# A two-layer hybrid decoder trunk: the small groups, the memory transposes and half the key projection of the mixer stage in another order

## The reference

```python
z = rmsnorm(x, mix_pre_g) @ w_in                 # 256 x 1024 @ 1024 x 3088
rq, rk, rv, rg, gq, gk, gv, ga, gg = split(z)
ro = retention(rope(rq), rope(rk) * 64**-0.5, rv)        # 4 heads, fixed decay, chunks of 128
ro = rmsnorm(ro) * silu(rg)
log_a = log_sigmoid(ga @ w_a2 + b_a2) / 16
go = gla(gq * 64**-0.5, gk, gv, log_a)                   # 4 heads, gated, causal
go = rmsnorm(go) * silu(gg)
x = x + rmsnorm(concat(ro, go) @ w_out, mix_post_g)

m = rmsnorm(mem, xa_mem_g)                               # 256 memory tokens
q = rmsnorm(x, xa_pre_g) @ w_q
k, v = split(m @ w_kv)                                   # 1024 columns each
x = x + rmsnorm(softmax(q k^T / 16) v @ w_o, xa_post_g)
```

## Time and profile before

| | |
|---|---|
| median of 3 executions | 1249.93 us (1248.46 to 1251.76) |
| the profiled execution, its own time | 1250.62 us |
| its span, first to last instruction | 1248.8 us |
| TensorE busy | 1214.5 us (97%) |
| VectorE busy | 801.1 us (64%) |
| ScalarE busy | 670.1 us (54%) |
| GpSimd busy | 153.7 us (12%) |
| mean granted clock of TensorE | 0.989 |

### The profile page before, as it was taken

One profiled execution on the slowest core, in us unless ns is written; L12 is line 12 of the kernel. 1 busy time (PEld: TensorE's weight loads), 2 busy tenths in 40 slices (PEclk: granted clock), 3 DMA queues, 4 the chain that ended last, 5 costly groups with the idle time before them and its releaser, 6 DMA issues.

```text
span 1248.8 us, 19448 instructions
## 1 busy us (share of the span) xinstructions
PE 1214.5 (97%) x6120; PEld 1017.2 (81%) x6120; DVE 801.1 (64%) x1214; ACT 670.1 (54%) x1117; POOL 153.7 (12%) x282
## 2 busy tenths in 40 slices
PE   7999999998999999999999999999899999999997
PEld 5888888777898888888888888877779988888886
DVE  6766546766756576665476665567667557767655
ACT  6655436644655466553466553456457546555444
POOL 1000003642210010000010000037322001000001
PEclk9999999989999999999999999998999999999999
DMA  8556564442563355565465565463345544555563
GB/s 332 199 172 217 182 212 164 135 135 106 183 201 129 123 191 194 176 211 192 157 204 194 174 211 191 158 214 103 102 169 163 168 159 135 203 175 195 180 213 130
DMA packets 32916, 220.06 MB, mean 176 GB/s; under 512 B 4272, under 2 KB 4528, under 8 KB 8768
## 3 DMA queue, kind: packets, MB, share of 16 engines
q1 hardware_dynamic: 32544, 218.98, 51.2%
q10 hardware_dynamic: 288, 0.02, 0.0%
HBM read 217.93 MB, written 1.05 MB: 175 GB/s over the span
## 4 chain that ended last, share of the span: by engine, by line
PE 89%; DVE 4%; issue 2%; POOL 2%; ACT 1%; DMA 1%; DVEq 0%; ACTq 0%; SPq 0%; POOLq 0%
PE acc L465 27%; PE acc L467 27%; PE acc L466 26%; PE tb L524 3%; DVE w_lo L1182 2%; PE mb L615 1%; PE acc L774 1%; PE mb L758 1%; DMA raw<-in_gu 1%; PE mb L711 1%; ACT w_hi L870 1%; DVE pg L1316 0%; POOL r_head L1679 0%; PE mb L713 0%; DVE xT_lo L1188 0%
## 5 line engine op out<-in xcount | busy, mean ns | idle before, releaser
L1182 DVE SCALAR_TENSOR_TENSOR w_lo<-raw,gains,w_hi 128x512 fp32r<-128x512 f32 x580 | 416.3, 779 | 46.5 <-ACT w_hi L870 45.4
L465 PE MATMUL acc<-w_hi,xT_hi 128*128 128x512 f32 x1024 | 411.3, 402 | 8.4 <-DVE w_lo L1563 4.0
L467 PE MATMUL acc<-w_hi,xT_lo 128*128 128x512 f32 x1024 | 402.7, 393 | 0.0
L466 PE MATMUL acc<-w_lo,xT_hi 128*128 128x512 f32 x1024 | 402.2, 393 | 0.0
L870 ACT ACTIVATE w_hi<-raw,gains 128x512 fp32r<-128x512 f32 x580 | 369.9, 714 | 40.4 <-PE acc L467 40.2
L465 PEld LDWEIGHTS acc<-w_hi,xT_hi 128*128 128x128 f32 x1024 | 194.4, 190 | 51.3 <-DVE xT_lo L1188 5.1
L467 PEld LDWEIGHTS acc<-w_hi,xT_lo 128*128 128x128 f32 x1024 | 194.1, 190 | 41.7
L466 PEld LDWEIGHTS acc<-w_lo,xT_hi 128*128 128x128 f32 x1024 | 194.6, 190 | 37.8
L1176 DVE TENSOR_TENSOR w_lo<-raw,w_hi 128x1024 fp32r<-128x1024 f32 x112 | 123.6, 1145 | 72.6 <-ACT w_hi L864 71.9
L935 ACT ACTIVATE th<-acc,r_half 128x256 f32<-128x256 f32 x88 | 41.7, 474 | 197.3 <-PE acc L467 196.9
L864 ACT ACTIVATE w_hi<-raw 128x1024 fp32r<-128x1024 f32 x112 | 105.4, 991 | 77.2 <-PE acc L467 77.2
(11 more groups left out here) (175 smaller groups left out, 1250.2 us busy)
## 6 DMA issues: line engine op xcount, KB each, us to landing
raw<-in_gu SPq DMA_DIRECT2D x92, 1024.0 KB, 5.2
raw<-in_down SPq DMA_DIRECT2D x32, 1024.0 KB, 5.0
raw<-in_in SPq DMA_DIRECT2D x24, 1024.0 KB, 5.1
raw<-in_kv SPq DMA_DIRECT2D x16, 1024.0 KB, 5.2
raw<-in_down SPq DMA_DIRECT2D x16, 768.0 KB, 4.1
raw<-in_out SPq DMA_DIRECT2D x8, 1024.0 KB, 5.1
raw<-in_q SPq DMA_DIRECT2D x8, 1024.0 KB, 5.2
raw<-in_o SPq DMA_DIRECT2D x8, 1024.0 KB, 5.1
```

Source lines behind the costliest of these rows:

```text
L465: pe.matmul(o, st_hi, mv_hi, start=first, stop=False)
L466: pe.matmul(o, st_hi, mv_lo, start=False, stop=False)
L467: return pe.matmul(o, st_lo, mv_hi, start=False, stop=last)
L1182: dve.scalar_tensor_tensor(w_lo[:, slot, k, :], raw[:, slot, k, :], gains[:, ds(g, 1)], w_hi[:, slot, k, :].bitcast(F32), ALU.mult, ALU.su ...
```

## The change

The work is the same, the order is another. In words:

- TensorE: from pass 4 to pass 9 there is one small group in the middle of a pass (at `k == 4`, so between its two halves) and one behind it. The retention scores come first, then the levels one by one. `ro` stands in the middle of pass 10, `go` behind it. The memory transposes stand inside pass 10. The mixed transposes go by group of heads and not by half of the tokens: retention's behind pass 11, gla's between the two column passes of the first half of the keys.
- One chunk of keys (`C_K0`) is taken ahead of `w_out`, the other (`C_K1`) stays behind it, with the transposes of the new x behind and inside its passes.
- VectorE's and ScalarE's lists follow: one `split_after` between two `level_out` mostly; the squares and the scaling of the memory tokens, and their splitting, come into the projection. GpSimd's `mem_norm` moves to between the levels.
- SyncE loads the memory tokens behind chunk `C_IN + 3`, when x is updated after the first block (`s_x`), into the buffer `yg`; `kT`, `qT` and the probabilities' buffer trade places in memory.

```diff
+C_K0 = len(CHUNKS)
+CHUNKS += [("kv", 0, 0, 4, G_MEM)]
 C_OUT = len(CHUNKS)
 CHUNKS += [("out", c, 0, 4, G_HEAD) for c in range(2)]
-C_K = len(CHUNKS)
-CHUNKS += [("kv", c, 0, 4, G_MEM) for c in range(2)]
+C_K1 = len(CHUNKS)
+CHUNKS += [("kv", 1, 0, 4, G_MEM)]
...
-T_USES += [("mix", t, a) for t, a in XUSE]
 T_USES += [("mem", t, a) for t, a in XUSE]
+T_USES += [("mix", t, a) for a in range(2) for t in range(TT)]
...
-M_USES = ["z", "diag", "lv0", "lv1", "lv2", "rj0", "lv3", "rj1", "lv4", "lv5", "ro", "lv6", "lv7", "go",
+M_USES = ["z", "diag", "rj0", "rj1", "lv0", "lv1", "lv2", "lv3", "lv4", "lv5", "lv6", "lv7", "ro", "go",
           "s0", "s1"]
...
-            kT = sb("kT", [P, KD, TOK], F32, region)
+            qT = sb("qT", [P, KD, TOK], F32, region)
             vx = sb("vx", [P, TT, D], F32, region)
-            mem_t = sb("mem_t", [P, TT, D], F32, region)
+            p_t = sb("p_t", [P, TT, D], F32, region)
...
+        mem_t = yg
...
-                    if ci == C_K:
-
-                        sp.wait_ge(s_of, l * 4 + 4)
-                        sp.dma_start(mem_t[:, :, :], a["mem"].rearrange("(t p) d -> p t d", p=P)).then_inc(s_mem, 16)
-                    if ci == C_K + 3:
+                    if ci == C_V:
                         load_post_gain(l, 2)
                     load(l, ci)
+                    if ci == C_IN + 3:
+
+                        sp.wait_ge(s_x, l * 16 + 8)
+                        sp.dma_start(mem_t[:, :, :], a["mem"].rearrange("(t p) d -> p t d", p=P)).then_inc(s_mem, 16)
...
+                inside = {4: {4: diagonal}, 5: {4: lambda: retention_scores(0)}, 6: {4: lambda: level(l, 0)},
+                          7: {4: lambda: level(l, 2)}, 8: {4: lambda: level(l, 4)}, 9: {4: lambda: level(l, 6)},
+                          10: {2: lambda: mem_transposes(l, 0), 4: retention_outputs,
+                               6: lambda: mem_transposes(l, 1)}}
+                behind = {4: rqk_transposes, 5: lambda: retention_scores(1), 6: lambda: level(l, 1),
+                          7: lambda: level(l, 3), 8: lambda: level(l, 5), 9: lambda: level(l, 7),
+                          10: gated_outputs, 11: lambda: mixed_transposes(l, 0)}
+                for n in range(4, 12):
+                    c, t = n // 2, n % 2
+
+                    def step(k):
+                        if k in inside.get(n, {}):
+                            inside[n][k]()
+                    chunk_pass(l, C_IN + c, Q_IN + c, t, xT_hi, xT_lo, before_k=step)
+                    behind[n]()
...
-                mixed_transposes(l, 0, (1,))
+                wait_split(("mem", 1, 1), l)
+                column_pass(l, C_K0, Q_K0, 0, mT_hi, mT_lo)
+                mixed_transposes(l, 1)
+                column_pass(l, C_K0, Q_K0, 1, mT_hi, mT_lo)
...
-                pair(l, C_OUT, (Q_OUT, Q_OUT + 1), (xT_hi, xT_lo), before_k={0: mix_split(0), 2: mix_split(1)},
-                     mids={0: lambda: mixed_transposes(l, 1), 1: lambda: mem_transposes(l, 0),
-                           2: lambda: mem_transposes(l, 1)})
-
-                wait_split(("mem", 1, 1), l)
-                for t in range(TT):
-                    column_pass(l, C_K, Q_K, t, mT_hi, mT_lo)
-                    x_transposes(l, 2, t)
-                for t in range(TT):
-                    column_pass(l, C_K + 1, Q_K + 1, t, mT_hi, mT_lo)
+                pair(l, C_OUT, (Q_OUT, Q_OUT + 1), (xT_hi, xT_lo), before_k={0: mix_split(0), 2: mix_split(1)})
+                column_pass(l, C_K1, Q_K1, 0, mT_hi, mT_lo)
+                x_transposes(l, 2, 0)
+                column_pass(l, C_K1, Q_K1, 1, mT_hi, mT_lo, mid=lambda: x_transposes(l, 2, 1))
                 wait_x(l, 2, 1)
```

ScalarE's list, from the second half of gla v on:

```diff
                 project(2, 1, v_tok[:, 1, COL:2 * COL], r_8)
                 split_after(5)
+                act.wait_ge(s_mem, l * 16 + 16)
+                for t in range(TT):
...
+                    act.activation(junk_x[:, :], mem_t[:, t, :], ACT.Square,
+                                   accum_out=mss[:, t:t + 1]).then_inc(s_msq, 1)
                 exp_decay(l, 4)
                 project(3, 0, v_tok[:, 0, 0:COL], r_pre)
...
                 exp_decay(l, 6)
-                gate_tanh(4, 0)
                 split_after(8)
                 exp_decay(l, 7)
+                gate_tanh(4, 0)
+                split_after(9)
+                gate_tanh(4, 1)
+                split_after(10)
+                mem_hi(l, 0)
                 head_outputs(l, "ro", 0)
-                gate_tanh(4, 1)
-                split_after(9)
+                mem_hi(l, 1)
+                gate_tanh(5, 0)
                 head_outputs(l, "go", 1)
...
+                split_after(11)
                 gate_tanh(5, 1)
...
+                mix_hi(l, 0)
+                split_hi(l, C_OUT, 1)
```

VectorE's list, from behind the diagonal on, and GpSimd's:

```diff
-                split_after(3)
-                split_after(4)
-                level_out(0)
-                level_out(1)
+                split_lo(l, C_IN + 3, 0, ks=(0, 1))
                 for t in range(TT):
                     t_copy(l, ("rqk", t), rT[:, :, t * P:(t + 1) * P])
+                split_lo(l, C_IN + 3, 0, ks=(2, 3))
+                retention_mask(0)
+                split_after(4)
+                retention_mask(1)
+                level_out(0)
                 split_after(5)
+                level_out(1)
+                split_after(6)
                 level_out(2)
-                split_after(6)
-                retention_mask(0)
+                split_after(7)
                 level_out(3)
-                split_after(7)
-                retention_mask(1)
-                gate_z(4, 0)
+                split_after(8)
                 level_out(4)
                 level_out(5)
-                split_after(8)
+                for t in range(TT):
+                    dve.wait_ge(s_rmem, l * 2 + t + 1)
+                    dve.tensor_scalar(mem_t[:, t, :], mem_t[:, t, :], r_mem[:, t:t + 1], None,
+                                      ALU.mult).then_inc(s_memn, 1)
+                gate_z(4, 0)
+                level_out(6)
+                split_after(9)
+                level_out(7)
+                gate_z(4, 1)
+                split_after(10)
+                mem_lo(l, 0)
                 head_squares("ro", 0)
-                gate_z(4, 1)
-                level_out(6)
-                level_out(7)
-                split_after(9)
+                mem_lo(l, 1)
+                gate_z(5, 0)
                 head_squares("go", 1)
                 for t in range(TT):
                     mixed(4, t)
...
+                split_after(11)
                 gate_z(5, 1)
...
+                mix_lo(l, 0)
+                for t in range(TT):
+                    mixed(5, t)
+                split_lo(l, C_OUT, 1)
...
                     decayed(l, n)
                     if n + 2 < 8:
                         exponents(l, n + 2)
+                    if n in (3, 4):
+                        mem_norm(l, n - 3)
```

More of the change, by code:

```diff
@@ L617, in level, with mixed_transposes @@
                                 mm.then_inc(s_m[e], 1)
-            def mixed_transposes(l, t, groups=(0, 1)):
-                for g in groups:
+            def mixed_transposes(l, g):
+                for t in range(TT):
                     pe.wait_ge(s_mixed, l * 4 + 2 * g + t + 1)
@@ L1073, in mix_out, with mem_hi, mix_hi, copy_out @@
                                    accum_out=mss[:, t:t + 1]).then_inc(s_msq, 1)
+                exp_decay(l, 4)
+                project(3, 0, v_tok[:, 0, 0:COL], r_pre)
+                split_after(6)
+                exp_decay(l, 5)
+                project(3, 1, v_tok[:, 1, 0:COL], r_pre)
+                split_after(7)
+                exp_decay(l, 6)
+                split_after(8)
+                exp_decay(l, 7)
+                gate_tanh(4, 0)
[3 more added lines that the diff above has]
+                mem_hi(l, 0)
+                head_outputs(l, "ro", 0)
+                mem_hi(l, 1)
+                gate_tanh(5, 0)
+                head_outputs(l, "go", 1)
+                split_after(11)
+                gate_tanh(5, 1)
+                mix_hi(l, 0)
+                split_hi(l, C_OUT, 1)
+            def mem_hi(l, t):
+                for g in range(2):
+                    t_hi(l, ("mem", t, g), mT_hi[:, 4 * g:4 * g + 4, t * P:(t + 1) * P])
+            def mix_hi(l, g):
+                for t in range(TT):
+                    t_hi(l, ("mix", t, g), xT_hi[:, 4 * g:4 * g + 4, t * P:(t + 1) * P])
+            def copy_out(l, q, t, dst):
+                wait_pass(l, q, t)
+                act.activation(dst, acc[q % 2][t][:, :], ACT.Copy).then_inc(s_accf[bank(q, t)], 1)
+            def mix_out(l):
+                copy_out(l, Q_K0, 0, kT[:, 0:2, :])
+                mix_hi(l, 1)
+                split_hi(l, C_OUT + 1, 0)
+                copy_out(l, Q_K0, 1, kT[:, 2:4, :])
+                split_hi(l, C_OUT + 1, 1)
                 y_square(l, 1, Q_OUT, 0, 0)
-                mem_hi(l, 0)
```

(24 more changed lines are left out.)

297 lines of the change are left out of this document (122 added, 175 removed).

## The result

The changed kernel takes **1229.3 us** (median of four executions, 1228.6 to 1229.7) against 1249.5 us for the kernel before on the same chip (1248.5 to 1251.8). The ratio is 0.9839, with a 95% interval of 0.9827 to 0.9851: 20 us faster. The forecast was 1226 us, in a range of 1221 to 1238 us.

A forecast was written before the change was run, and what follows sets the result against it. TensorE, busy 97% of the span, was taken as the bound. From 1250.6 us, 17.3 us idle and 11 us clock go, 4.0 us of new waits come, 0.7 us off for the median: 1226 us, range 1221 to 1238 us.

The forecast's parts named there:

- What was to be won: In the mixer stages of both layers: 17.3 us of TensorE's idle time plus 11 us of clock, at most 28.3 us.
- Which waits go: TensorE's waits of 1.95, 1.23 and 1.76 us per layer, shorter ones among the groups, `xT_lo` (1.73 us) and `mem_t` (0.6 us).
- Two prices: VectorE's scaling of the memory tokens at 2 x 0.75 us, and one `level_out` per step at 0.79 us.
- The new waits: TensorE ahead of levels 0, 3 and 4: 0.2 + 0.3 + 1.5 = 2.0 us per layer, none from level 5 on.
- The clock: In the mixer stages, the 11 us lost at the lower clock were all to go, with none lost anew.
- groups set apart by half a pass keep it: Between passes 4 and 10: small groups with half a pass between them keep full clock; a wait among small groups costs it.
- The sum: 17.3 us idle and 11 us clock go, 2 x 2.0 us come: 24.3 us off 1250.6 us; 1225.6 us as median.
- A: Rival: clock still falls behind the new wait ahead of level 4, or in pass 10; 11 us stay, 1237 us; chance 0.15.
- B: Rival: VectorE bounds the mixer stage, 5 us of waits a layer, no clock lost: 1232 us; chance 0.20.
- C: Rival: the chopped stretch, passes 4 to 11, runs at half clock and the kernel gets slower: 1280 us; chance 0.04.
- D: Rival: VectorE's splits and GpSimd's instructions exclude each other fully, 13 us of waits a layer: 1248 us; chance 0.03.

The follow-up runs named there:

- Kernel 2: The changed kernel with level_out(3) moved ahead of split_after(7) and level_out(4) ahead of split_after(8) in VectorE's list: 1222.2 us, ratio 0.9788.
- experiment 5: The changed kernel with w_out's two chunks ahead of both key chunks, as in the kernel before; new order of small groups and memory tokens kept: 1239.4 us.
- experiment 3: The changed kernel with split_after(7) ahead of project(3, 1) in ScalarE's list, VectorE's list as it was: 1224.8 us, ratio 0.9804.
- experiment 6: The changed kernel with GpSimd's instructions from level 2 on cut to the first block of each decayed operand, leaving out computation: 1224.2 us, ratio 0.9809.
- experiment 4: The changed kernel with level 4 behind pass 8, next to level 5, and no group inside pass 8: 1230.1 us, ratio 0.9846.
- experiment 8: The kernel before with level_out(0) moved between split_after(3) and split_after(4) in VectorE's list, nothing else: 1242.4 us, ratio 0.9955.
- experiment 7: Kernel 2 with TensorE made to wait ahead of w_out's second and fourth pass until the pass before has been read: 1235.3 us, ratio 0.9903.
- experiment 1: The changed kernel with only level_out(3) moved ahead of split_after(7) in VectorE's list: 1231.3 us, ratio 0.9859.

## Why the prediction was nearly right, point by point

- **What was to be won: right.** It said 17.3 + 11 = 28.3 us. Kernel 2, which loses nothing in the stage, ends 28.3 us earlier by its span, with 16.9 us of idle time and 11.4 us of busy time, which is the clock's. The terms are off by 0.4 us each, and that they cancel to the decimal is luck.
- **Which waits go: right.** `pgx`, `xT_lo` and `mem_t` are gone, and the banks of `ro` and level 7 are waited for no more, nor are GpSimd's operands of level 0. `xT_lo` went because of the key chunk (experiment 5). The squares, the scaling and the memory transposes cost nothing that TensorE shows: kernel 2 has them all and no wait. Two prices were off without effect: the scaling ran beside GpSimd at 1.0 us an instruction and not 0.75 us, and `level_out` of levels 6 and 7 took 1.33 us and not 0.79 us.
- **The new waits: right in sum and at level 4, wrong in the small ones.** Forecast 4.0 us, measured 2.6 + 1.9 = 4.5 us. At level 4 it was 1.9 us a layer where 1.5 us was worked out, by the named cause, ScalarE's projection (experiment 3), together with the splits' slowing beside GpSimd (experiment 6). The 0.2 and 0.3 us ahead of levels 0 and 3 did not come; 0.67 us at level 5 came in layer 0, where "no more waits" was forecast, since four splits took 4.19 us there.
- **The clock: this term was mis-sized.** It was put at nothing, and the step that failed is "groups set apart by half a pass keep it". The fall behind level 4 in layer 1 came with half a pass ahead of the group and half a pass behind it; its window lacks 25 x 0.07 = 1.7 us. Against kernel 2 the changed one is busy 1205.5 - 1203.1 = 2.4 us longer, so the clock gave back at least 9.0 us of its 11.4 us; the 0.7 us that the window doesn't show were not placed. The reason under that step, that a wait costs the clock when it stands among small groups, does not hold as a rule: the same neighbourhood gave a fall in one layer and none in the other (experiment 4). What it is worth as a tendency is said below. Kernel 2, which has no wait in the stage, has no fall there.
- **The sum.** 0.5 us more of waits and 2.4 us more of busy time make 2.9 us: 1250.6 - 28.3 + 4.5 + 2.4 = 1229.2 us, and the profiled execution took 1229.1 us. The 0.7 us that was taken off for the median fell away, since this time the profiled execution lay 0.2 us below the median. Together that is the distance of 3.7 us between 1225.6 and 1229.3 us.
- **The rivals.** A (1237 us) came true behind one of the three waits that were left, and at a fifth of its price. B (1232 us, waits in every step) did not: levels 0 to 3 did not wait. C is refuted by the mean clock of 0.998. D is refuted as it was priced: no 13 us of waits came.

**What D had wrong is its price.** It added 2.7 us of splits and GpSimd's 3.5 us a level to 6.2 us. But the 3.5 us holds GpSimd's own waiting for VectorE, so the blocking was counted twice. The two timelines of the changed kernel show it:

```profile
259.06 0.73 POOL L1672 TENSOR_TENSOR gqk<-gT,o_sb 128x256 f32<-128x256 f32 x1
...
262.25 0.87 POOL L1671 TENSOR_TENSOR gqk<-gT,o_sb 128x256 f32<-128x256 f32 x1
262.46 1.22 DVE L1183 SCALAR_TENSOR_TENSOR w_lo<-raw,gains,w_hi 128x512 fp32r<-128x512 f32 x1
263.09 1.17 POOL L1672 TENSOR_TENSOR gqk<-gT,o_sb 128x256 f32<-128x256 f32 x1
263.60 1.21 DVE L1183 SCALAR_TENSOR_TENSOR w_lo<-raw,gains,w_hi 128x512 fp32r<-128x512 f32 x1
```

A split takes 0.74 us when GpSimd is quiet and 1.2 us here; a GpSimd instruction takes 0.73 us without splits beside it and 1.17 us here. They end in turn, at 263.13 (GpSimd), 263.68, 264.26 (GpSimd) and 264.81 us, each 0.55 to 0.58 us behind the other. Four such rounds are 4 x 1.13 = 4.5 us, an estimate from these rows, and the longest four splits measured took 4.43 us. The page "SBUF — State Buffer" of the Trainium skill (section "SBUF: two separate sides") has the two exclude each other instruction by instruction. The trace agrees with such turns; it was the sum of 6.2 us, and not the rule, that the time refuted.

**What stays open** is what decides whether a given wait lowers the clock. The profiled executions give these counts for waits of 1.2 to 2.4 us. Directly behind another small group, 7 of 10 were followed by a fall: of those of 1.23 us 2 of 4 (before yes, experiment 8 no), of those of 1.76 us 4 of 4 (the same two kernels), of those of 2.3 us 1 of 2 (experiment 4). With large matmuls on both sides it was 2 of 8: at level 4 one of two in the changed kernel and one of two in experiment 5, in the other layer; in experiment 7 none of four. The waits of 2.9 us and 3.3 us had a fall in both layers. So length alone doesn't order the cases, and small groups next to a wait seem to make a fall likelier without deciding it. These are few cases, from one execution of each kernel, and no run isolates either.

## What to carry to other kernels

Price a wait of the bound engine by more than its length: here 17 us of waits came with 11 us lost by the lower clock, and the 4.5 us that were left came with 2.4 us more of busy time. When lists are written by hand, put the short instruction that frees a bank ahead of the long block that nobody is waiting for yet, and look for the engine one step further back: here VectorE's splits waited for ScalarE's, and these stood behind an operation that TensorE gated. And when a new order has a step of VectorE longer than TensorE's (4.8 against 4.0 us here), see where its slack ends: moving one instruction only moved the wait (experiment 1), moving both removed it (experiment 2).

## What the runs showed of the hardware that was not expected

- The clock's answer to the same wait at the same place differs between layers and between executions: in experiment 7 four executions of one kernel had a mean clock of 0.998, 0.994, 0.997 and 0.994 and times of 1232.6 to 1238.2 us. A single profile of such a kernel can show none of its falls.
- Large matmuls on either side of a wait don't keep the clock for certain: half passes stood on both sides of level 4 in layer 1, where it fell behind a wait of 1.90 us.
- VectorE and GpSimd take turns where both work on such operands, at 0.55 to 0.58 us each, so both get slower, and a time read beside the other engine is not an engine's own. The two copies of `level_out` at levels 1 to 5 of layer 0 kept their 0.75 to 0.77 us together, beside GpSimd too. Four splits of VectorE beside GpSimd took 3.56 to 4.43 us against 2.74 us with a light GpSimd; the 4.43 us is from kernel 2, in layer 0:

```profile
266.06 4.43 DVE L1183 SCALAR_TENSOR_TENSOR w_lo<-raw,gains,w_hi 128x512 fp32r<-128x512 f32 x4
```
